# Input map's upper powers from ScalarE's turned copies, six modulation units ahead of its first block, and the first output quarter ahead of the phases

## What is computed

```python
mod = silu(c) @ w_ada[i] + b_ada[i]            # 6 sections of 1024: shift, scale, gate, ...
h = modulate(rms_norm(x, norm_g[i, 0]), sh1, sc1)
# s5_mixer, per group of 16 channels with 64 complex states:
ab = exp(a * dt)                                # complex, by magnitude, cos, sin
bb = ((ab - 1) / a) * b                         # complex input matrix
state[t] = ab * state[t-1] + bb @ u[t]
y[t] = real(c @ state[t]) + d * u[t]
```

## Time and profile before

| | us |
|---|---|
| median of three runs | 1039.05 |
| lowest and highest | 1038.18, 1040.37 |
| the profiled execution | 1038.83 |
| its span, first to last instruction | 1036.9 |

### The profile page before, as it was taken

The page is one execution under the profiler, slowest core; times in us unless marked ns, Lnnn a source line. Parts: engine busy times, 40 slices in busy tenths (PEclk is TensorE's granted clock), DMA queues, the critical chain, the costliest instruction groups (busy, mean ns, idle before and its releaser), DMA issues.

```text
span 1036.9 us, 16695 instructions
## 1 busy us (share of the span) xinstructions
PE 957.9 (92%) x6354; PEld 800.8 (77%) x6355; DVE 855.3 (82%) x1119; ACT 635.1 (61%) x787; POOL 55.6 (5%) x116
## 2 busy tenths in 40 slices
PE   0685799899999999999999999999999999999995
PEld 0464588899999979767888888888888888888884
DVE  7989985498777856995778998989989898998994
ACT  4436274544433445774477868778686786867762
POOL 4002300010000001001000000000000000000000
PEclk9987899999999999999899999999999999999998
DMA  9897694699989759602479999999999999999961
GB/s 240 333 344 187 140 324 142 240 341 353 315 275 314 276 188 353 210 34 78 148 264 356 333 397 313 377 376 327 401 316 384 364 337 389 314 387 347 356 248 63
DMA packets 134242, 297.64 MB, mean 287 GB/s; under 512 B 9494, under 2 KB 40843, under 8 KB 133915
## 3 DMA queue, kind: packets, MB, share of 16 engines
q1 hardware_dynamic: 126026, 282.92, 76.1%
q0 software_dynamic: 4080, 8.48, 3.0%
q10 hardware_dynamic: 4064, 5.26, 1.8%
HBM read 291.06 MB, written 3.16 MB: 284 GB/s over the span
## 4 chain that ended last, share of the span: by engine, by line
PE 82%; DVE 13%; ACT 3%; issue 1%; DMA 1%; ACTq 0%; SPq 0%; DVEq 0%
PE ps L643 24%; PE ps L645 24%; PE ps L644 24%; PE ps L1183 1%; PE ps L727 1%; PE ps L1042 1%; PE ps L1156 1%; PE ps L1157 1%; ACT s_low_turned L1444 1%; DVE s_out_map L1943 1%; PE ps L1134 1%; PE ps L744 1%; DMA mod_rows<-ada_wide 0%; DVE s_g L2001 0%; PE ps L1051 0%
## 5 line engine op out<-in xcount | busy, mean ns | idle before, releaser
L2332 DVE TENSOR_TENSOR w_lo<-raw,w_hi 128x2048 fp32r<-128x2048 f32 x162 | 365.7, 2288 | 36.5 <-ACT w_hi L1637 36.5
L1637 ACT ACTIVATE w_hi<-raw 128x2048 fp32r<-128x2048 f32 x162 | 303.0, 1913 | 0.0
L643 PE MATMUL ps<-w_hi,xe_hi 128*128 128x512 f32 x448 | 177.6, 396 | 1.3 <-DVE xe_lo L2292 1.3
L645 PE MATMUL ps<-w_hi,xe_lo 128*128 128x512 f32 x448 | 175.3, 391 | 0.0
L644 PE MATMUL ps<-w_lo,xe_hi 128*128 128x512 f32 x448 | 174.6, 390 | 0.0
L1736 DVE TENSOR_TENSOR w_lo<-raw,w_hi 128x2048 fp32r<-128x2048 f32 (+3 forms) x59 | 131.6, 2249 | 28.8 <-ACT w_hi L1308 27.8
L1308 ACT ACTIVATE w_hi<-raw 128x2048 fp32r<-128x2048 f32 (+3 forms) x59 | 108.7, 1874 | 11.1 <-DMA raw<-in_mla_w_in 6.2
L643 PE MATMUL ps<-act_hi,w_hi 128*128 128x256 f32 x352 | 100.5, 286 | 1.9 <-DVE act_lo L1904 1.9
L645 PE MATMUL ps<-act_hi,w_lo 128*128 128x256 f32 x352 | 99.6, 283 | 0.0
L644 PE MATMUL ps<-act_lo,w_hi 128*128 128x256 f32 x352 | 99.6, 283 | 0.0
L643 PEld LDWEIGHTS ps<-w_hi,xe_hi 128*128 128x128 f32 x448 | 84.2, 188 | 18.3 <-issue 1.5
(11 more groups left out here) (430 smaller groups left out, 1563.3 us busy)
## 6 DMA issues: line engine op xcount, KB each, us to landing
raw<-in_moe_w_in SPq DMA_DIRECT2D x112, 1024.0 KB, 6.9
raw<-in_moe_w_out SPq DMA_DIRECT2D x56, 1024.0 KB, 8.0
raw<-in_w_ada SPq DMA_DIRECT2D x48, 1024.0 KB, 7.7
raw<-in_ffn_w_in SPq DMA_DIRECT2D x44, 512.0 KB, 6.7
raw<-in_ffn_w_out SPq DMA_DIRECT2D x11, 1024.0 KB, 7.7
raw<-in_ssm_w_glu SPq DMA_DIRECT2D x16, 512.0 KB, 7.4
raw<-in_mla_w_o SPq DMA_DIRECT2D x4, 1024.0 KB, 8.6
raw<-in_mla_w_uq SPq DMA_DIRECT2D x3, 768.0 KB, 7.2
```

The costliest lines, as they stand in the source:

```text
L643: mm(dst, st[0], mv[0], start=first, stop=False)
L645: return mm(dst, st[1], mv[0], start=False, stop=last)
L1637: af(HI[:, (V_MOE + m) % RING, :], RAW[:, (RAW_OF_W[V_MOE] + m) % RING, :], cp).then_inc(hi_done, 1)
L2332: tt_(LO[:, slot, :], RAW[:, (RAW_OF_W[V_MOE] + m) % RING, :], HI[:, slot, :].bitcast(F32), ALU.subtract)\
```

## The change

Four things are changed, all in the state-space part.

The input map is built in four quarters of eight pairs, as the output map is. `r_base(d)` makes the four lower powers by the six VectorE operations of 512 elements; `r_turned(d)` on ScalarE writes the turned copies into a new tile `RTD`, 16 activations of 64 elements; `r_high(d)` makes the four upper powers by eight fused operations. The quarters have four places, of which the first and the last are the same (148 KB). A quarter feeds two rounds.

On TensorE six units, `c_rows` and `norm_0` stand ahead of round 0. Rounds 2 to 6 and the modulation columns are ordered anew, and round 7 stands behind the shuffle and unit 12.

On ScalarE the turned copies stand among the copies out of PSUM, and the third and fourth `zero_map` stand behind all of these.

On VectorE the first output quarter stands ahead of the phases. New waits: `r_base(2)` for the transposed output matrix, `r_base(3)` for round 1, the first output quarter for round 5, the phases for round 7.

```diff
-        RBLKS = [at("s5_rblk_a", [P, 2, 4, L, GH], 180), at("s5_rblk_b", [P, 2, 4, L, GH], 143)]
+        RBLKS = [at(f"s5_rblk_{n}", [P, 2, 8, L, GH], kb) for n, kb in zip("abcd", (148, 188, 116, 148))]
+        RTD = at("s5_rblk_turned", [P, 2, 8, 2, 4 * GH], 124)
...
-        TURN = at("s5_turns", [P, 3, 8, GI], 112)
+        TURN = at("s5_turns", [P, 3, 8, GI], 143)
...
             def r_round(r):
 
+                pe.wait_ge(rblk_ok, r // 2 + 1)
                 for c in range(2):
                     n = 2 * r + c
-                    pe.wait_ge(rblk_ok, n + 1)
...
-            r_round(0)
-            ada(0)
-            ada(1)
-            c_rows()
+            for n in range(4):
+                ada(n)
+            c_rows()
+            ada(4)
+            norm_0()
+            ada(5)
+            r_round(0)
             r_round(1)
-            ada(2)
-            ada(3)
-            norm_0()
-            r_round(2)
-            ada(4)
-            ada(5)
-            r_round(3)
             ada(6)
             ada(7)
+            r_round(2)
+            r_round(3)
+            mod_columns(0)
+            mod_columns(1)
             r_round(4)
             r_round(5)
-            mod_columns(0)
-            mod_columns(1)
+            r_round(6)
             for n in range(8, 11):
                 ada(n)
             shuffle_inputs()
             ada(11)
             ada(12)
-            r_round(6)
+            r_round(7)
             ada(13)
             ada(14)
-            r_round(7)
...
+            def r_turned(d):
+
+                act.wait_ge(o_low, 2 * d + 2)
+                if d >= 2:
+                    act.wait_ge(rblk_ok, d - 1)
+                for k in range(8):
+                    gi = 8 * d + k
+                    for c in range(2):
+                        last = af(RTD[:, d % 2, k, c, :], RBLKS[d][:, 1 - c, k, 4:8, :].rearrange("p t h -> p (t h)"), cp,
+                                  scale=PW[:, 0, gi, 8:9] if c == 0 else PW[:, 1, gi, 4:5])
+                last.then_inc(o_turn, 1)
+
+            r_turned(0)
+            for c in range(2):
+                act.wait_ge(ct_ps, c + 1)
+                af(CT[:, c, :, :].rearrange("p g h -> p (g h)"), PS[:, c, :], cp).then_inc(ct_ok, 1)
+            wide(0)
+            r_turned(1)
+            for n in range(4):
                 rt_copy(n)
...
+            wide(1)
+            r_turned(2)
+            for n in range(4, 8):
+                rt_copy(n)
+            r_turned(3)
+            for n in range(8, 12):
+                rt_copy(n)
...
+            for n in range(12, 14):
+                rt_copy(n)
...
+            for n in range(14, 16):
+                rt_copy(n)
+            zero_map(2)
+            zero_map(3)
             wide(2)
...
+            def r_base(d):
+
+                if d == 2:
+                    dve.wait_ge(ct_ps, 2)
+                if d == 3:
+                    dve.wait_ge(rt_ps, 4)
+                if d:
+                    dve.wait_ge(o_low, 2 * d)
+                sh, g = [P, 8, 4, GH], slice(8 * d, 8 * d + 8)
+                p = [PWR[:, c, g, 4:8].unsqueeze(3).broadcast_to(sh) for c in range(2)]
...
+            def r_high(d):
+
+                dve.wait_ge(o_turn, d + 1)
+                dve.wait_ge(o_low, 2 * d + 2)
+                for k in range(8):
+                    gi = 8 * d + k
+                    last = stt(out=RBLKS[d][:, :, k, 0:4, :].rearrange("p c t h -> p c (t h)"),
+                               in0=RBLKS[d][:, :, k, 4:8, :].rearrange("p c t h -> p c (t h)"), scalar=PW[:, 0, gi, 4:5],
+                               in1=RTD[:, d % 2, k, :, :], op0=ALU.mult, op1=ALU.add)
+                last.then_inc(rblk_ok, 1)
...
-            r_block(0)
+            r_base(0)
             norm_rows(0, XN0, XN0)
-            for r in range(1, 6):
-                r_block(r)
+            r_base(1)
+            r_high(0)
+            r_base(2)
+            r_high(1)
+            r_base(3)
             mod_rows(0)
             mod_rows(1)
             mod_columns(0)
             mod_columns(1)
-            for r in range(6, 8):
-                r_block(r)
-
-            dve.wait_ge(rblk_ok, 16)
+            r_high(2)
+            r_high(3)
+
+            dve.wait_ge(ct_ok, 2)
+            dve.wait_ge(rblk_ok, 4)
+            dve.wait_ge(rt_ps, 12)
+            o_base(0)
+            dve.wait_ge(o_low, 10)
+            dve.wait_ge(rt_ps, 16)
             v_.memset(TAB[:, 0, :, 0:1], 1.0)
...
-            dve.wait_ge(ct_ok, 2)
-            dve.wait_ge(rt_ps, 16)
             for j in range(4):
-                o_base(j)
+                if j:
+                    o_base(j)
```

More of the change, by code:

```diff
@@ L1409, in gelus @@
                 af(AH[:, dt:dt + 2, :], H32[:, dt:dt + 2, :], cp).then_inc(zh_ok, 1)
-            for n in range(16):
-                rt_copy(n)
[L1413 to L1430, removed]
-                    act.wait_ge(u_ps, 1)
-                    for r in range(4):
-                        af(U[:, :, :].rearrange("p (d g) j -> p g d j", g=8)[:, 2 * r:2 * r + 2, :, :],
-                           PS[:, r, :].rearrange("p (a d j) -> p a d j", a=2, d=DT), cp).then_inc(u_ok, 1)
@@ new lines, in _ @@
+            act.wait_ge(mod_ok, 2)
+            for dt in range(DT):
+                act.wait_ge(n_ps, dt // 2 + 1)
+                af(UT[:, dt, :, :], PS[:, dt // 2, (dt % 2) * SEQ:(dt % 2 + 1) * SEQ].rearrange("p (j t) -> p t j", t=L),
+                   ACT.Identity, bias=MOD[:, 0, dt:dt + 1], scale=MOD[:, 1, dt:dt + 1]).then_inc(n_f32, 1)
+            for n in range(12, 14):
+                rt_copy(n)
+            act.wait_ge(u_ps, 1)
+            for r in range(4):
+                af(U[:, :, :].rearrange("p (d g) j -> p g d j", g=8)[:, 2 * r:2 * r + 2, :, :],
+                   PS[:, r, :].rearrange("p (a d j) -> p a d j", a=2, d=DT), cp).then_inc(u_ok, 1)
@@ L1437, in _ @@
             for j in range(4):
-                act.wait_ge(o_low, 2 * j + 2)
+                act.wait_ge(o_low, 8 + 2 * j + 2)
                 if j >= 2:
@@ L1834, in _ @@
             dve.wait_ge(bb_ok, 1)
[L1836 to L1840, removed]
-                if r >= 2:
-                    dve.wait_ge(rt_ps, 2 * r - 2)
-                sh = [P, 4, L, GH]
-                p = [PWR[:, c, g, :].unsqueeze(3).broadcast_to(sh) for c in range(2)]
+            def r_base(d):
[7 more added lines that the diff above has]
+                p = [PWR[:, c, g, 4:8].unsqueeze(3).broadcast_to(sh) for c in range(2)]
                 b = [BB[:, c, g, :].unsqueeze(2).broadcast_to(sh) for c in range(2)]
-                o = [RBLKS[r % 2][:, c, :, :, :] for c in range(2)]
-                t = [RTMP[:, i, :].rearrange("p (g t h) -> p g t h", g=4, t=L) for i in range(2)]
+                o = [RBLKS[d][:, c, :, 4:8, :] for c in range(2)]
+                t = [RTMP[:, i, :].rearrange("p (g t h) -> p g t h", g=8, t=4) for i in range(2)]
                 tt_(o[0], p[0], b[0], ALU.mult)
@@ L1937, in o_high @@
             def o_high(j):
-                dve.wait_ge(o_turn, j + 1)
-                dve.wait_ge(o_low, 2 * j + 2)
+                dve.wait_ge(o_turn, 4 + j + 1)
+                dve.wait_ge(o_low, 8 + 2 * j + 2)
                 for k in range(8):
```

9 lines of the change are left out of this document (4 added, 5 removed).

## The result

| | before | after |
|---|---|---|
| median, us | 1038.89 (16 runs, 1037.81 to 1040.37) | 1040.84 (16 runs, 1039.87 to 1043.74) |
| ratio | | 1.0023, 95% interval 1.0017 to 1.0030 |
| the profiled execution | 1038.83 | 1043.74 |
| its span | 1036.9 | 1041.8 |
| PE, DVE, ACT busy | 957.9, 855.3, 635.1 | 964.8, 848.5, 650.0 |

The kernel became slower by 0.23%, some 2.4 us (1.95 as the difference of the medians). The forecast was 3.6 us, so the direction came out, and two thirds of the size (little over half of it by the medians). The profiled execution happens to be the longest of its 16, so its dates are read within the stage and its end is not. VectorE works 6.8 us less and ScalarE 14.9 us more, near the prices (7.1 and 15.7).

The account below looks back on a forecast made before the run. VectorE was taken to bound the rebuilt state-space stage, TensorE nearly everything behind it. A second output quarter 3.84 us late, less 0.20, added 3.64 to 1038.83: 1042.5 us, own range 1041.2 to 1044.5, 8-in-10 range 1038.2 to 1045.6.

Parts of the forecast that it names:

- VectorE 7.1 us less, ScalarE more in front of its copies: Input map in quarters: VectorE does 7.1 us less; ScalarE gets 15.7 us more, not hidden, ahead of its PSUM copies.
- Units ahead cost and bring nothing: TensorE before round 0: units moved early fit into idle time between 21 and 36 us, effect 0.
- The normed input cold: TensorE's sixteen transposes of the normed input, from 36.1 us, run at the low clock and take 3.9 us.
- The stall behind turned 2, and the clock behind it: TensorE idles 4.5 us, 46.7 to 51.25, for ScalarE's copy behind turned 2; round 3 then runs at the low clock.
- The columns, high 3, UT, tail: Modulation columns done 55.2, high 3 ended 60.0, UT copies 62.1 to 65.9, then shuffle, units and round 7 by 71.7.
- One date among the unknowns: Clock behind 51 us: if high throughout, round 3 and the modulation columns end at 52.5.
- The new wait and the quarter that fills it: VectorE's phases wait for round 7; the first output quarter fills part, then VectorE idles 6.3 us until 71.75.
- The sum: Second output quarter +3.84 us (82.26 for 78.42), less 0.20 of vanished waits: +3.64 us, 1042.5 in total.
- the carry-over: Whatever the state-space stage gains or loses moves all later stages by the same amount.
- The break-even of 67.9: Round 7 done at 67.9 us means no change; each microsecond sooner is one gained, down to 61.7.
- the tie: Rival, 25%: TensorE's clock stays high or rises early in rounds 3 to 6; 1038.0 to 1041, centre 1039.0.
- rival "faster": Rival, 12%: VectorE's 7.1 us count and round 7 is not last; priced at 3 us, 1035.8.

Follow-up runs that it names:

- e6: The kernel before with units 0 to 5 and the transposed output matrix ahead of round 0 on TensorE, nothing else: 1038.57 us, ratio 0.9995.
- e3: The kernel after with ScalarE's PSUM copies 4 to 7 moved ahead of turned 2: 1039.66 us, ratio 1.0006 to before.
- e5: The kernel after with 18 useless 128x128 matmuls on TensorE between rounds 2 and 3: 1040.06 us, ratio 1.0008 to before.
- e4: The kernel after with the first output quarter moved back behind the phases on VectorE: 1045.72 us, ratio 1.0060 to before.
- e14: The kernel after, unchanged, run and profiled a second time: 1040.82 us, ratio 1.0022 to before.
- e1: The kernel after with round 7 directly behind round 6 and ScalarE's copies 12 and 13 ahead of the UT copies: 1040.79 us, ratio 1.0014 to before.
- e7: e1 plus copies 4 to 7 ahead of turned 2, and the first turned output quarter in its own tile, ahead of the shuffled-input copies: 1038.54 us, ratio 0.9997 to before.
- e2: The kernel after with 32 useless 128x128 matmuls on TensorE between rounds 2 and 3: 1045.86 us, ratio 1.0063 to before.
- e8: e7 with the first strips ahead of units 16 to 19 on TensorE: 1044.94 us, ratio 1.0045 to before.
- e13: e8 with SyncE's transfer of the first strips' rows put ahead in its queue of weight loads: 1042.74 us, ratio 1.0034 to before.
- e15: The kernel after with ScalarE's copies 4 to 7 ahead of turned 2 and 18 useless matmuls behind round 3: 1040.11 us, ratio 1.0009 to before.

## Why the prediction was right, and where it was off

**VectorE 7.1 us less, ScalarE more in front of its copies: right.** 6.8 measured, and none of it reached the end. A group of turned copies took 3.93 us, as the output map's. The Trainium skill, "VectorE: DVE Perf Modes", TRN2 errata, makes it 3.84 by an estimate from its fixed cost per operation; the trace agrees within 0.1.

**Units ahead cost and bring nothing: right** (e6).

**The normed input cold: half right.** It took 3.27 where I had 3.9 and the high clock gives 1.97: the granted clock was 0.50 from 36 to 38 and 1.00 again in 39 to 40, so it rose on the way. Nor had it been low all along, as I had it: the unit at 32.23 took 1.07, the high clock, and the level fell again while TensorE waited 2.85 us for CT. The first unit came at 19.63, not 20.8, and moved nothing.

**The stall behind turned 2, and the clock behind it: right.** 4.65 us for a forecast of 4.5, from 46.0 instead of 46.7; round 3 at the low clock. e3 and e5 show each to be a part of the date: 1.3 us for the order, 1.8 for the clock, 2.1 together.

**The columns, high 3, UT, tail: right, each date 0.6 to 1.0 us early.** The columns were stored at 54.4 (55.4), high 3 waited 0.38 us for turned 3 and started at 57.04 (57.8), UT began at 61.08 (62.1), round 7 released the phases at 71.08 (71.7). The mis-sized term is the sum of small ones: turned 2 started 0.6 sooner, behind the shorter normed input, and both columns took 1.86 together, not 2 x 1.01. One date among the unknowns was summed wrongly, with no effect: at the high clock round 3 and the columns would end at 53.3 (51.25 + 1.04 + the 1.05 that e5 shows), not at 52.5, but turned 3 ends last there anyway.

**The new wait and the quarter that fills it: right.** 6.50 us for a forecast of 6.3; e4 prices the filling at 3.8 to 4.9.

**The sum: right in sign, too large by a third.** The second quarter came 3.18 us late, not 3.84, since round 7 was done 0.67 sooner than I had it (71.08 for 71.75). This is the mis-sized term. Of 3.18 the third quarter kept 2.90 (0.20 of the difference is the wait of the earlier trace rows, as said), and the operation behind the map 2.85, in e14 2.3. The ratio gives 2.4 us, with an interval from 1.8 to 3.1. So for this kernel the carry-over, "moves everything behind it by the same amount", stands within the noise.

It does not stand for larger shifts. e1 and e7 started the phases 6.1 and 7.1 us sooner than after, and their ratios are lower by 0.0009 and 0.0026, some 0.9 and 2.7 us. Most of that was lost before the end of the map, where they were 2.0 and 3.1 us ahead: VectorE waited for ScalarE's turned copies, which in turn waited for TensorE. By the date behind the map (the table's third column) the ratios of all kernels but four follow within 1.2 us. Of the 8.4 and 7.8 us of e2 and e4 they show 6.5 and 6.2, and e8 and e13, 2 us early there, lost 3.5 to 4.7 us on before by the transfers and halts told above. The break-even of 67.9 was not refuted: e3, e5 and e15, with phases from 68.96 to 69.76, lie at 1.0006 to 1.0009, all with intervals that hold 1. But under it, in e1 and e7, nothing more was gained.

**The result stands at the edge that I drew.** The ratio is above 1.002, the median of 1040.84 just under the 1041.1 that I set from the three runs of before, and outside the forecast's own range (from 1041.2), inside the whole one. What decides that it was the forecast's case and not the tie is the mechanism: the clock did not stay high (0.50 in 51 to 54), and where it was kept high for longer (e5, e15) the loss was no longer clear of the noise.

**Of the rival "faster":** no kernel is clear of before on the fast side. Removing the wait (e1), and ScalarE's late copies with it (e7), gives a tie, so that rival was priced too well: what was late next in e7 stood on TensorE, at the strips, where I had said "no cost".

**The hand-over.** The profiled execution lost another 2 us behind the map that the median doesn't show. TensorE's timeline ahead of the first projection matmul, before:

```profile
128.80 3.34 PE L727 MATMUL ps<-ident 128*128 128x128 f32 x18
132.19 0.77 PE L643 MATMUL ps<-w_hi,act_hi 128*128 128x512 f32 x1
```

After:

```profile
131.12 1.01 PE L709 MATMUL ps<-ident,mod_rows 4*128 4x4 f32 x4 [3.69 <-DVE mod_rows L1893]
132.06 4.21 PE L728 MATMUL ps<-ident 128*128 128x128 f32 x18
135.93 0.77 PE L644 MATMUL ps<-w_hi,act_hi 128*128 128x512 f32 x1
```

3.74 us late there, 0.9 of it the same 18 transposes at a lower clock (4.21 against 3.34). e14 has the same:

```profile
131.49 4.21 PE L728 MATMUL ps<-ident 128*128 128x128 f32 x18
135.35 0.77 PE L644 MATMUL ps<-w_hi,act_hi 128*128 128x512 f32 x1
```

So the clock at the hand-over is low in both executions, against e14's expectation that it differs from run to run; in e1 and e7 the 18 transposes took 2.27. I had no term for it. Both executions are longer than the median of their kernel, so whether the usual one has it isn't shown. That the clock explains the rest of the 4.9 us of the first span, of which 1.2 lie behind the first projection matmul, is argued from these rows, not shown by a run.

## What to carry to other kernels

An operation moved from the busiest engine to an idle one is paid in the order of the idle one: look what stands behind it there, and who waits for that, before counting the saving. Where a tile takes over the memory of another, the wait that guards it has a date of its own; work it out through all engines, and put independent work in front of it (here 3.9 us of work were worth 3.8 to 4.9 us). And before counting saved time on one engine as gained, find the second-latest chain: here a lead of 4.2 us for VectorE shrank to 0.25 us at the next hand-over from TensorE and ScalarE.

## What the runs showed of the hardware

- TensorE's halts with the releaser "issue" are waits for its own instructions, as far as dates show it: each of 39 such halts (0.3 to 5.69 us) ends 1.25 to 2.20 us behind a 16 KB packet on the queue "q8 instruction", and they stand at fixed places of the program. They were 3.20 us at 122.46 in e1, 4.91 in e8, 5.69 and 2.67 in e13. In before there is none at the first of those two places, ahead of which TensorE had waited 2.13 us for VectorE's states, and one of 0.27 near the second. What sets the start of the packet is open.
- A 128x128 matmul of f32 is recorded twice, 0.114 us each (7.31 us for 64 records of 32 matmuls), so a filler is twice as long as its count suggests. A transpose of that size is recorded once.
- The clock column is not to be trusted ahead of the first full stretch of matmuls: one unit of after took 1.94 us at 19.63, where the windows say 1.00, and at 67.95 two units took 1.93. Durations decide.
- Eighteen matmuls of no use, laid in a hole of 4.65 us, were worth 1.8 us on the path, since round 3 and the columns behind them then ran at the high clock (1.06 and 1.05 us instead of 1.94 and 1.86).
